# Output projection: three row tiles share one pass over k, the gate row and the second chunk's z are issued earlier, the finish is one multiply-add, the last tile goes in halves

## The reference: what is computed

```python
z = jnp.concatenate([y_lru * silu(g_lru), y_pool * silu(g_pool), y_conf * silu(g_conf)], axis=-1)
o_x = jnp.einsum('bnm,md->bnd', z, w_out)                 # 2048 x 1024 by 1024 x 1024
x = x + gt_x[:, None, :] * rmsnorm(o_x, g_post)           # x already holds the position embedding
```

## Time and profile before

| what | us |
|---|---|
| three executions | 850.33, 852.43, 852.49 |
| median | 852.43 |
| the profiled execution, its own time | 854.36 |
| the profiled execution, span from first to last instruction | 852.3 |
| TensorE busy in the span | 771.0 |
| mean granted TensorE clock, share of full speed | 0.953 |

### The profile page before, as it was taken

How to read it: one execution, slowest core, us unless ns; L and a number is a source line. 1 busy time by engine, 2 the same in 40 slices (tenths; PEclk the granted TensorE clock), 3 DMA queues, 4 the chain that set the end, 5 groups by cost and what they waited for, 6 DMA issues and landing times.

```text
span 852.3 us, 9918 instructions
## 1 busy us (share of the span) xinstructions
PE 771.0 (90%) x3468; PEld 616.6 (72%) x3468; DVE 539.0 (63%) x748; ACT 456.3 (54%) x749; POOL 342.9 (40%) x373
## 2 busy tenths in 40 slices
PE   6695899899889896999879997999999799999996
PEld 2275787688678785888758885777777488888885
DVE  4389763648866889399966554657615476666632
ACT  4264742697846963887944882343425243434311
POOL 0258653455544452535551466222210224242421
PEclk9797999999999997999998999899999999999998
DMA  9994014235424245234533234344337965857531
GB/s 365 357 302 152 25 38 126 59 90 164 146 74 144 77 145 159 94 116 145 168 108 105 68 101 145 90 132 137 111 111 277 302 211 176 273 171 261 178 124 77
DMA packets 89073, 130.09 MB, mean 153 GB/s; under 512 B 22752, under 2 KB 54112, under 8 KB 87488
## 3 DMA queue, kind: packets, MB, share of 16 engines
q1 hardware_dynamic: 84656, 115.44, 41.8%
q0 software_dynamic: 4368, 14.03, 6.2%
HBM read 91.17 MB, written 38.27 MB: 152 GB/s over the span
## 4 chain that ended last, share of the span: by engine, by line
PE 62%; DVE 11%; DMA 7%; ACT 6%; issue 5%; SPq 5%; POOL 4%; DVEq 0%; POOLq 0%; ACTq 0%
PE bank L1455 20%; PE bank L1456 19%; PE bank L1457 19%; SPq L418 2%; DMA scratch_u<-ustage 2%; DVE xc L1116 2%; PE bank L1483 1%; DMA wm<-in_w_mod 1%; DVE Qb L1262 1%; PE bank L1463 1%; DMA gb<-scratch_u 1%; DVE xTl L1167 1%; POOL spl L675 1%; DMA vbuf<-scratch_u 1%; DVE Ib L1252 1%
## 5 line engine op out<-in xcount | busy, mean ns | idle before, releaser
L1455 PE MATMUL bank<-xTh,wh 128*128 128x512 f32 (+1 forms) x592 | 235.0, 397 | 6.7 <-DVE wl L1142 4.1
L1457 PE MATMUL bank<-xTh,wl 128*128 128x512 f32 (+1 forms) x592 | 232.1, 392 | 0.0
L1456 PE MATMUL bank<-xTl,wh 128*128 128x512 f32 x576 | 228.4, 397 | 0.0
L1455 PEld LDWEIGHTS bank<-xTh,wh 128*128 128x128 f32 x592 | 114.3, 193 | 30.8 <-DVE wl L1142 4.7
L1457 PEld LDWEIGHTS bank<-xTh,wl 128*128 128x128 f32 x592 | 113.7, 192 | 24.0
L1456 PEld LDWEIGHTS bank<-xTl,wh 128*128 128x128 f32 x576 | 110.9, 192 | 23.1 <-issue 0.2
L1455 PE MATMUL bank<-xTh 128*128 128x512 f32 (+1 forms) x272 | 106.5, 391 | 13.6 <-DVE xTl L1400 7.1
L1457 PE MATMUL bank<-xTh,xTl 128*128 128x512 f32 x256 | 99.9, 390 | 0.0
L1456 PE MATMUL bank<-xTl,xTh 128*128 128x512 f32 x256 | 99.7, 390 | 0.0
L917 ACT ACTIVATE ustage<-bank 128x512 f32<-128x512 f32 x56 | 33.2, 594 | 117.2 <-PE bank L1457 101.7
L590 POOL TENSOR_SCALAR sph<-xc 128x512 fp32r<-128x512 f32 (+1 forms) x36 | 26.8, 760 | 118.7 <-PE bank L1457 88.6
(11 more groups left out here) (188 smaller groups left out, 1486.3 us busy)
## 6 DMA issues: line engine op xcount, KB each, us to landing
scratch_u<-ustage SPq DMA_DIRECT2D x72, 256.0 KB, 3.2
wraw<-in_w_in SPq DMA_DIRECT2D x18, 512.0 KB, 4.6
wm<-in_w_mod SPq DMA_DIRECT2D x8, 1024.0 KB, 11.7
xg<-in_x SPq DMA_DIRECT2D x16, 512.0 KB, 8.6
yb<-scratch_y SPq DMA_DIRECT2D x32, 256.0 KB, 3.0
gb<-scratch_u SPq DMA_DIRECT2D x32, 256.0 KB, 4.3
xres<-in_x SPq DMA_DIRECT2D x16, 512.0 KB, 4.8
out<-tout SPq DMA_DIRECT2D x16, 512.0 KB, 3.0
```

Of the source, the lines that this page charges most:

```text
L1455: mm(out, wh_, xh_, start=first, stop=False)
L1456: mm(out, wh_, xl_, start=False, stop=False)
L1457: return mm(out, wl_, xh_, start=False, stop=last)
```

## The change

It edits only the order and the form of the last part, in seven places.

1. Tiles 0, 1 and 2 are computed together: k is the outer loop, and under each k stand the three tiles with their two halves (18 matmuls). They use the bank pairs 2-3, 4-5 and 0-1, so PE waits for the last unit's copy out of banks 0 and 1 first. Tile 3 takes banks 6-7.
2. Four bank pairs rotate in place of three. Tile n >= 4 waits for the read of tile n - 4; tile 3 waits until the gate row has been used.
3. The gate row is computed behind unit -3, in banks 6-7.
4. In `TAIL`, items 0 and 1 and wo 4 stand behind unit -3, item 2, wo 5, item 3 and wo 6 behind unit -2, wo 7 and items 4 to 7 behind unit -1. SP issues wo 0 to 3, items 0 to 2 and then wo 4 to 7.
5. The second chunk's items stand ahead of tile 0 in `STAGE5`.
6. The finish multiplies bank by `gbc` in each half as soon as that half's squares are done, and then makes (tout * rr2) + xres in one instruction.
7. The last tile runs its halves one after the other over all k, with its own count for each; its multiply-add and its store go in two halves.

```diff
-        ob = [bank[2:4], bank[4:6], bank[6:8]]
-        gob = bank[0:2]
+        ob = [bank[2:4], bank[4:6], bank[0:2], bank[6:8]]
+        gob = bank[6:8]
...
-        side = [("wo", k) for k in range(KD)] + [("item", k) for k in range(KD)]
+        BEHIND = [[("wo", k) for k in range(4)], [("item", 0), ("item", 1), ("wo", 4)],
+                  [("item", 2), ("wo", 5), ("item", 3), ("wo", 6)], [("wo", 7)] + [("item", k) for k in range(4, KD)]]
         while rest:
             TAIL.append(rest.pop(0))
-            behind = 0 if TAIL[-1][1] < HALF_DONE else 4 if TAIL[-1][1] < THREE_DONE else 3
-            TAIL += side[:behind]
-            side = side[behind:]
-        TAIL += side
+            TAIL += BEHIND.pop(0) if len(rest) < 4 else []
...
-        STAGE5 = []
+        TOGETHER = 3
+        STAGE5 = [("item", KD + k) for k in range(KD)]
         for n, (c, i) in enumerate(TILES):
             STAGE5.append(("tile", n))
-            if c + 1 < NCH:
+            if 0 < c < NCH - 1:
                 STAGE5 += [("item", (c + 1) * KD + m) for m in range(3 * i, min(3 * i + 3, KD))]
...
                 sp.wait_ge(s_of, n + 1)
-                sp.dma_start(out[n * P:(n + 1) * P, :], tout[:, n % 2, :]).then_inc(s_out[n % 2], 16)
+                if n + 1 < len(TILES):
+                    sp.dma_start(out[n * P:(n + 1) * P, :], tout[:, n % 2, :]).then_inc(s_out[n % 2], 16)
+                    return
+                for h in range(2):
+                    hs = slice(h * CH, (h + 1) * CH)
+                    sp.wait_ge(s_of, n + 1 + h)
+                    sp.dma_start(out[n * P:(n + 1) * P, hs], tout[:, n % 2, hs]).then_inc(s_out[n % 2], 16)
...
                     if n == HALF_DONE:
-                        for k in range(KD):
+                        for k in range(4):
                             load_wo(k)
                         for k in range(3):
                             load_item(k)
+                        for k in range(4, KD):
+                            load_wo(k)
...
                     for h in range(2):
-                        a.activation(sqj[:, h * CH:(h + 1) * CH], ob[m % 3][h][:], ACT.Square,
+                        act.wait_ge(s_om, products(m, h))
+                        a.activation(sqj[:, h * CH:(h + 1) * CH], ob[m % 4][h][:], ACT.Square,
                                      accum_out=ss2[:, h:h + 1]).then_inc(s_osq, 1)
...
-                    dve.wait_ge(s_osq, 2 * n + 2)
-                    v.tensor_tensor(out=ssum, in0=ss2[:, 0:1], in1=ss2[:, 1:2], op=ALU.add).then_inc(s_oss, 1)
-                    dve.wait_ge(s_ort, n + 1)
-                    link(v.reciprocal(rr2, rs2))
                     if n >= 2:
                         dve.wait_ge(s_out[n % 2], 16 * (n // 2))
                     for h in range(2):
                         hs = slice(h * CH, (h + 1) * CH)
-                        ins = stt(tout[:, n % 2, hs], ob[n % 3][h][:], rr2, gbc[:, hs], ALU.mult, ALU.mult)
-                    ins.then_inc(s_ot, 1)
-                    dve.wait_ge(s_ot, n + 1)
+                        dve.wait_ge(s_osq, 2 * n + h + 1)
+                        if h:
+                            v.tensor_tensor(out=ssum, in0=ss2[:, 0:1], in1=ss2[:, 1:2], op=ALU.add).then_inc(s_oss, 1)
+                        v.tensor_tensor(out=tout[:, n % 2, hs], in0=ob[n % 4][h][:], in1=gbc[:, hs],
+                                        op=ALU.mult).then_inc(s_ot, 1)
+                    dve.wait_ge(s_ort, n + 1)
+                    link(v.reciprocal(rr2, rs2))
+                    dve.wait_ge(s_ot, 2 * n + 2)
                     dve.wait_ge(s_xp, 2 * n + 2)
-                    v.tensor_tensor(out=tout[:, n % 2, :], in0=tout[:, n % 2, :], in1=xres[:, n % 2, :],
-                                    op=ALU.add).then_inc(s_of, 1)
+                    last = n + 1 == len(TILES)
+                    for cols in ((slice(0, CH), slice(CH, D)) if last else (slice(0, D),)):
+                        stt(tout[:, n % 2, cols], tout[:, n % 2, cols], rr2, xres[:, n % 2, cols],
+                            ALU.mult, ALU.add).then_inc(s_of, 1)
...
                 if kind == "unit":
                     unit(n)
+                    if n == THREE_DONE:
+                        gate_row()
...
             pe.wait_ge(s_lye, 2 * NCH)
...
+            pe.wait_ge(s_ev, N_CU + len(UNITS))
+            for k in range(KD):
+                pe.wait_ge(s_zl, k + 1)
+                pe.wait_ge(s_wol, k + 1)
+                for n in range(TOGETHER):
+                    for h in range(2):
+                        ins = product(n, k, h)
+                    if k == KD - 1:
+                        ins.then_inc(s_om, 1)
+            for n in range(TOGETHER, len(TILES)):
+                c, i = TILES[n]
+                if n == 3:
+                    pe.wait_ge(s_gbc, 1)
+                else:
+                    pe.wait_ge(s_ot, 2 * (n - 3))
+                if n + 1 == len(TILES):
+                    for h in range(2):
+                        for k in range(KD):
+                            ins = product(n, k, h)
+                        ins.then_inc(s_om, 1)
+                    continue
                 for k in range(KD):
                     if i == 0:
                         pe.wait_ge(s_zl, KD * c + k + 1)
-                    if n == 0:
-                        pe.wait_ge(s_wol, k + 1)
                     for h in range(2):
...
+                        ins = product(n, k, h)
                 ins.then_inc(s_om, 1)
-                if n == 0:
-                    gate_row()
```

More of the change, by code:

```diff
@@ L300, in mixer_kernel @@
         s_wor, s_woh, s_wol = [sem(f"wo_in{k}") for k in range(KD)], sem("wo_hi"), sem("wo_lo")
-        s_gmm, s_gpo = sem("gate_product"), sem("gpost_in")
+        s_gmm, s_gpo, s_gbc = sem("gate_product"), sem("gpost_in"), sem("gate_row_ready")
         s_wg, s_ga = sem("wgate_in"), sem("gate_summed")
@@ L304, in mixer_kernel @@
         s_sg, s_z, s_zh, s_zl = sem("gate_silu"), sem("z_ready"), sem("z_hi"), sem("z_lo")
-        s_om, s_osq, s_ort, s_ot = sem("out_product"), sem("out_squares"), sem("out_root"), sem("out_scaled")
+        s_om, s_osq, s_ort, s_ot = sem("out_product"), sem("out_squares"), sem("out_root"), sem("out_weighted")
         s_xr = [sem(f"xres_in{b}") for b in range(2)]
@@ L394, in mixer_kernel, with products @@
         HALF_DONE, THREE_DONE = PROJ_AT[-5], PROJ_AT[-3]
-        side = [("wo", k) for k in range(KD)] + [("item", k) for k in range(KD)]
+        BEHIND = [[("wo", k) for k in range(4)], [("item", 0), ("item", 1), ("wo", 4)],
+                  [("item", 2), ("wo", 5), ("item", 3), ("wo", 6)], [("wo", 7)] + [("item", k) for k in range(4, KD)]]
         while rest:
             TAIL.append(rest.pop(0))
-            behind = 0 if TAIL[-1][1] < HALF_DONE else 4 if TAIL[-1][1] < THREE_DONE else 3
-            TAIL += side[:behind]
-            side = side[behind:]
-        TAIL += side
+            TAIL += BEHIND.pop(0) if len(rest) < 4 else []
         ITEMS = [(c, k) for c in range(NCH) for k in range(KD)]
         TILES = [(c, i) for c in range(NCH) for i in range(TPC)]
-        STAGE5 = []
+        def products(n, h):
+            return n + 1 + h if n + 1 == len(TILES) else n + 1
+        TOGETHER = 3
+        STAGE5 = [("item", KD + k) for k in range(KD)]
         for n, (c, i) in enumerate(TILES):
             STAGE5.append(("tile", n))
-            if c + 1 < NCH:
+            if 0 < c < NCH - 1:
                 STAGE5 += [("item", (c + 1) * KD + m) for m in range(3 * i, min(3 * i + 3, KD))]
@@ L580, in _ @@
             for b in range(2):
-                sp.wait_ge(s_out[b], 16 * len(TILES) // 2)
+                sp.wait_ge(s_out[b], 16 * (len(TILES) // 2 + b))
         @block.gpsimd
@@ L1090, in _ @@
                 else:
-                    act.wait_ge(s_om, m + 1)
                     if m:
@@ L1427, in _ @@
                 link(stt(gbc[:, hs], gob[h][:], 256.0, gbc[:, hs], ALU.mult, ALU.add))
-                link(v.tensor_tensor(out=gbc[:, hs], in0=gbc[:, hs], in1=gpo[:, hs], op=ALU.mult))
+                ins = v.tensor_tensor(out=gbc[:, hs], in0=gbc[:, hs], in1=gpo[:, hs], op=ALU.mult)
+                if h == 0:
+                    link(ins)
+                else:
+                    ins.then_inc(s_gbc, 1)
+                    dve.wait_ge(s_gbc, 1)
             for kind, n in STAGE5:
@@ L1551, in _, with gate_row @@
             assert q == STEPS
+            def gate_row():
+                pe.wait_ge(s_ga, KD)
+                pe.wait_ge(s_pye, 2 * NCH)
+                for h in range(2):
+                    mm(gob[h][:], onesk[:], gacc[:, h * CH:(h + 1) * CH], start=True, stop=True).then_inc(s_gmm, 1)
             for kind, n in TAIL:
@@ L1591, in _, with product @@
                     mm3(pmb[n % 2][:], pwh[:, i, :], pwl[:, i, :], pdh[:], pdl[:], True, True).then_inc(s_pmm, 1)
-            pe.wait_ge(s_lye, 2 * NCH)
[L1594 to L1606, removed]
```

(28 more changed lines are left out.)

2 lines of the change are left out of this document (removed).

## The result

The changed kernel took 843.32 us, the median of four executions (842.19 to 844.24), against 851.88 (850.33 to 852.49) for the kernel before in the same comparison: 8.6 us less, a ratio of 0.990 with a 95% interval of 0.9885 to 0.9915. The forecast was 840.3, within 837.3 and 843.7, so the time lies in the range and near its upper end. It lies outside the forecast's own narrower range, 838.5 to 841.5, and inside the band of the rival of a late copy, 841.3 to 843.5. Two more comparisons later (e1, e12) gave 9.9 and 10.8 us less. The gain is real, and smaller than the 12.1 forecast by 3.5, 2.2 and 1.3 us.

The account below looks back on a forecast made before the run. TensorE was taken to bound tiles 1 to 15, with 11.0 us lost before them to waits and low clock. Savings of 10.1 (reordering), 1.4 (finish) and 0.6 (store), 12.1 us, off 852.43 gave 840.3 us, range 837.3 to 843.7.

Parts of the forecast that it names:

- the forecast's own narrower range: Whole kernel: 838.5 to 841.5 us from the bounds of start, finish, store and scatter; held 75 in 100.
- the rival of a late copy: Group's start: item 3 lands after 657.5, delaying ACT's last copy 1 to 3 us; 841.3 to 843.5 us, 12 in 100.
- the milder rivals: Late copy at the group's start (12 in 100) and tile 4 waiting for its banks (6 in 100); they end at 844.
- a wrong first step: PE's timeline behind the last unit: one gap of 0.9 us was forecast; over 2 us would show the step wrong.
- Tile 0 starves, three tiles under one k don't: Tile 0's slices of six matmuls (1.4 us) starve at 2.44 us per item; slices of 18 (4.08 us) have no wait.
- The start S: Group's first product on PE at 660.1 us; new wait for the last unit's copy costs 0.9 us, bounds 0.25 and 3.9.
- 11.0 us are lost: PE from 657.48 to 844.46: 186.98 us less 174.3 and 1.72, lost to waits and low clock; most that reordering can give.
- The cover of tile 4: Tile 4, starting at 703.7 us, needs tile 0's finish, due 697 to 706: no wait expected, far bound 2.5 us.
- The finish and the store: Behind the last matmul: finish 3.34 us in place of 4.70, saving 1.4; last store of 256 KB saves 0.6, bounds 0 and 1.3.
- The sum: Whole kernel: 10.1 from PE's earlier end, 1.4 from the finish and 0.6 from the store, 12.1 us off.
- The clock rival: Three-tile group starves at every slice and runs at low clock: kernel slower, 873 us at worst; 3 in 100.

Follow-up runs that it names:

- e1: The changed kernel again, unedited, timed against the kernel before: 841.72 us, 9.9 less (0.989).
- e12: The changed kernel a third time, unedited, timed against the kernel before: 842.76 us, 10.8 less (0.9888).
- e6: The changed kernel with a group of one tile in place of three: 846.92 us, 5.7 less than the kernel before (0.9932).
- e7: The changed kernel with a group of two tiles in place of three: 842.20 us, 10.4 less than the kernel before (0.988).
- e4: The changed kernel with the old order of weights and items in TAIL and of their loads on SP: 840.52 us, 11.1 less than the kernel before (0.9878).
- e9: The changed kernel with SP's old load order alone, the other engines' lists left new: 843.78 us, 9.8 less than the kernel before (0.9888).
- e2: The kernel before with only the new finish and the last tile in halves: 850.30 us, 1.3 less than the kernel before (0.9985).
- e8: The kernel before, unchanged, for one more profile: one execution, 854.45 us.
- e5: The changed kernel with the second chunk's eight items back behind tiles 0, 1 and 2: 851.86 us against 852.60 for the kernel before (0.9996).
- e10: The changed kernel with its last tile in one piece and one store: 843.65 us, 9.9 less than the kernel before (0.9887).
- e3: The changed kernel with PE's wait for the last unit's copy put behind tiles 0 and 1 of slice 0: 840.00 us, 11.6 less than the kernel before (0.9879).
- e11: The version of e3 once more, beside the changed kernel: 841.30 us, 12.2 less than the kernel before (0.9862).

## Why the prediction was right, and where its sizes were off

The number lies in the range by the room that was added for the milder rivals: the forecast as worked out ended at 841.5. The sign that I had named for a wrong first step, a gap of over 2 us, came true in the first profile (2.06). The mechanism of the gain was right; the start of the group and the base were mis-sized.

**Tile 0 starves, three tiles under one k don't.** Right. The waits for items are gone at every slice, and the group of one tile (e6) brings four of them back. The cover that I named (items at a pace of 2.44 us against slices of 4.08) was larger than needed: two tiles do it (e7), and the old order of the first chunk's items does it too (e4). The fourth bank pair and the gate row's new place were not undone by themselves, so what each gives alone is open.

**The start S, "I take 0.9, and keep 0.25 and 3.9".** This is the mis-sized term. In the three profiles of the changed kernel the gap was 2.06, 0.82 and 1.81 us, 1.56 in the mean. The rival "a late copy holds the group's start" came true in two of three. In the first profile its cause was not the one I gave: unit -4's store, which the new load order delays by about 1.5 us (e9), held unit -2's copy, and behind it stood 3.43 us of ACT's work. Item 3's SiLU did not wait. In e12 both causes add up: the last copy began at 661.07, 1.1 us behind the last unit's end at 659.94, and 0.76 of it (4.19 - 3.43) is the wait for item 3, the cause that I gave. I had taken the store's 10.33 us over unchanged, and had item 3 landing near 656. I also left out that a gap of this length can drop the clock, 1.6 us more in one profile of three (e12); the earlier trace rows had shown such a drop behind an idle PE.

**"11.0 us are lost", the base.** 1.7 us of this was the low clock on the gate row in the one profiled execution: the pair lasted 3.33 us there and 1.88 in e2 and e8, and the matmuls next to it were slow too. With e8's P of 196.6 beside the first 197.8 the mean to save from is 0.6 us smaller. The step that failed is that I took a clock dip for a property of the kernel.

**The cover of tile 4.** I forecast no wait and it holds. But I gave the second chunk's move no weight of its own, and the gain depends on it: without it P is 197.0 (e5). The finish of three tiles that are done within 3 us of each other, put ahead of the items, gives back in tile 4 what the group saved.

**The finish and the store, 1.4 and 0.6.** T fell by 2.24 us against 2.0 forecast, and to 5.6 in every profile with both edits. Split by e10: 1.1 the new form of the finish, 1.2 the halves with their store.

**The sum.** The mean P + T is 205.1 over the two profiles of before (205.7, 204.5) and 194.7 over the three of the changed kernel (194.6, 193.4, 196.0): 10.4 us, with 0.2 lost outside the span (below) 10.2. The three comparisons gave 8.6, 9.9 and 10.8 us, 9.7 in the mean. Against 12.1: 0.6 from the base, 0.65 from the gap (1.56 - 0.9), 0.55 from the clock (1.6 in one of three), 0.2 outside the span, less 0.2 of a better tail, 1.8 in all. The rest of 0.6 us is within the scatter of the medians.

**The clock rival.** Its condition, waits between the slices, was not met, and the group ran at 1.00 apart from the dip behind the gap in e12. e5 met it, in tile 4: waits of 1.43 and 3.94 us between slices, then a granted clock of 0.50. The rule of the Trainium skill (TensorE: Matmul & The Clock Gate, HAM oscillation — how this bites in real kernels) asks for no wait between k-slices, since the clock falls each time. The traces agree with it in e5 and, behind a wait of 1.80 us, in the first profile of before. They don't bear out "each time": four waits between slices of up to 1.55 us (e6) and seven of up to 1.82 (e2) and 1.93 (e8) left the granted clock at 1.00. And the rule does not speak against k outermost as such, where no wait arises. What decides is the time of one slice against the pace of the data.

## What to carry to other kernels

If a product starves because its operand comes slice by slice, put so many output tiles under one slice that its matmuls last longer than one slice takes to arrive, and then look at what the joined finishes are queued ahead of: here undoing that queue alone (e5) cost the whole gain, and undoing the grouping alone (e6) less than half of it. Put a wait where its buffer is first used, not ahead of the whole group: moving one line (e3, e11) made P 186.7 us both times, against 187.8 to 190.4 in the changed kernel, and the medians 1.7 and 1.5 us lower, with overlapping intervals. Before taking idle or slow time in one profile for something to be won, look at a second profile, above all for a low clock.

## What the runs showed of the hardware that was not expected

- A gap of about 2 us on PE behind a long busy stretch was followed by some 3.4 us at the 1.2 GHz level in e12 (gap 1.81) and e7 (2.18), and was not in the first profile of the changed kernel (2.06), nor behind the gap at the same place in the first profile of before (1.81), in e8 (1.93) and in e2 (2.52), nor behind shorter ones (0.73 to 1.32, in e1, e4, e5, e6, e9 and e10). The length of the gap alone does not tell which; what does is not shown.
- The last tile in halves, with two stores at the very end, costs time that the span doesn't show. Device time less span is 1.83 to 1.88 us in the mean of 10 to 17 executions of the kernel before in each set, and 1.84 over the six of e10, which also ends in one store. The changed kernel's three sets have 2.07, 2.05 and 2.12, e2's twelve 2.07 and e5's twelve 2.09, the other kernels with halves 1.94 to 2.10. All that differs at the end between the changed kernel and e10 is the last tile in halves, with its two stores; why this costs time outside the span is not shown. It takes back 0.2 us of the 1.2 that the halves gain.
- The order of eight 512 KB and six 256 KB loads, their number unchanged, moved the landing of a store issued behind them by about 1.5 us (7.6 to 8.6 against 9.0 to 10.5 us for the copy that waits for it).
